# Seven block products for the value half of the first feed-forward too, and the key/value norm four tiles later

## What is computed

```
up = x @ w_up                      # (tokens, 1024) @ (1024, 2*2816)
u, val = up[..., :2816], up[..., 2816:]
c = conv_b + sum_j conv_w[j] * u_shifted[j]        # width 3
f = (gelu(c) * val) @ w_down       # (tokens, 2816) @ (2816, 1024)
h = h + rms_norm(f, g_ffn_post)
```

## Time and profile before

| | |
|---|---|
| median of three runs | 2568.37 us (2568.36 to 2572.23) |
| the profiled execution, its own time | 2568.32 us |
| its span, first to last instruction | 2566.5 us |
| mean granted TensorE clock | 0.986 of full |
| PE busy | 2434.8 us, 95% |
| DVE busy | 1752.6 us, 68% |
| ACT busy | 1190.4 us, 46% |
| down products of pass f = 0 | from 614.63 us |
| down products of pass f = 1 | from 988.29 us |
| down products of pass f = 2 | from 1810.88 us |
| down products of pass f = 3 | from 2181.33 us |

### The profile page before, as it was taken

One profiled execution on the slowest core, in us unless ns is written; L12 is line 12 of the kernel. 1 busy time (PEld: TensorE's weight loads), 2 busy tenths in 40 slices (PEclk: granted clock), 3 DMA queues, 4 the chain that ended last, 5 costly groups with the idle time before them and its releaser, 6 DMA issues. The chain is left out here.

```text
span 2566.5 us, 38650 instructions
## 1 busy us (share of the span) xinstructions
PE 2434.8 (95%) x15615; PEld 2140.6 (83%) x15615; DVE 1752.6 (68%) x3158; ACT 1190.4 (46%) x1884; POOL 44.1 (2%) x66
## 2 busy tenths in 40 slices
PE   7999999989999999999998899989899999999996
PEld 4777989877888889999996677767788889999996
DVE  5667576676766556766656655665888887787777
ACT  4655454454343334343325766764534544433343
POOL 0000000000000000000000000000000000000000
PEclk9999999999999999999999999989999999999998
DMA  4222223332433332423323242221333333233322
GB/s 160 66 66 91 83 79 108 120 108 88 161 102 117 105 99 89 134 75 99 109 83 92 96 126 64 85 79 54 92 116 134 99 99 99 84 106 124 99 91 98
DMA packets 88205, 255.24 MB, mean 99 GB/s; under 512 B 12963, under 2 KB 30540, under 8 KB 86092
## 3 DMA queue, kind: packets, MB, share of 16 engines
q1 hardware_dynamic: 68956, 202.45, 24.9%
q0 software_dynamic: 5792, 28.05, 3.4%
q10 hardware_dynamic: 13280, 22.28, 2.6%
HBM read 225.93 MB, written 26.74 MB: 98 GB/s over the span
## 5 line engine op out<-in xcount | busy, mean ns | idle before, releaser
L513 PE MATMUL banks<-act_hi,w_lo 128*128 128x272 f32 (+1 forms) x2520 | 834.5, 331 | 18.9 <-DVE act_lo L2634 7.3
L513 PE MATMUL banks<-act_hi,w_hi 128*128 128x272 f32 (+1 forms) x2520 | 819.8, 325 | 0.0
L513 PE MATMUL banks<-act_lo,w_hi 128*128 128x272 f32 (+1 forms) x2520 | 818.3, 325 | 0.0
L490 ACT ACTIVATE w_hi<-w_raw 128x1024 fp32r<-128x1024 f32 x366 | 382.5, 1055 | 575.2 <-PE banks L536 302.0
L496 DVE TENSOR_TENSOR w_lo<-w_raw,w_hi 128x1024 fp32r<-128x1024 f32 x366 | 444.2, 1221 | 235.9 <-ACT w_hi L490 235.6
L513 PEld LDWEIGHTS banks<-act_hi,w_lo 128*128 128x128 f32 x2520 | 477.3, 189 | 74.0 <-issue 24.6
L513 PEld LDWEIGHTS banks<-act_lo,w_hi 128*128 128x128 f32 x2520 | 478.0, 190 | 36.5 <-issue 1.7
L513 PEld LDWEIGHTS banks<-act_hi,w_hi 128*128 128x128 f32 x2520 | 476.7, 189 | 37.5
L548 DVE TENSOR_TENSOR acc<-acc,banks 128x272 f32<-128x272 f32 (+1 forms) x624 | 314.3, 518 | 182.8 <-PE banks L536 180.4
L536 PE MATMUL banks<-h_hi,w_lo 128*128 128x272 f32 (+1 forms) x1056 | 346.9, 328 | 21.9 <-DVE w_lo L496 8.3
L536 PE MATMUL banks<-h_lo,w_hi 128*128 128x272 f32 (+1 forms) x1056 | 345.4, 327 | 0.0
(11 more groups left out here) (275 smaller groups left out, 3430.3 us busy)
## 6 DMA issues: line engine op xcount, KB each, us to landing
w_raw<-wall SPq DMA_DIRECT2D x366, 512.0 KB, 3.5
normed<-h_scratch POOLq DMA_DIRECT2D x20, 352.0 KB, 4.1
h_scratch<-acc POOLq DMA_DIRECT2D x3, 2176.0 KB, 7.9
h_scratch<-acc POOLq DMA_DIRECT2D x3, 2048.0 KB, 7.8
gstates<-state ACTq DMA_DIRECT2D x4, 1024.0 KB, 6.4
gla_s<-gstates ACTq DMA_DIRECT2D x4, 1024.0 KB, 7.1
bias<-bias_scratch ACTq DMA_DIRECT2D x28, 128.0 KB, 2.9
bias_scratch<-bias_rows ACTq DMA_DIRECT2D x8, 383.0 KB
```

Source lines behind the costliest of these rows:

```text
L490: nc.scalar.activation(WH[:, b % RING, 0:n], raw(b), ACT.Copy).then_inc(w_hi, 1)
L513: last = nc.tensor.matmul(PS[:, bank, 0:n], w, a[X][:, k, o:o + n], start=(k == 0 and first), stop=(k == KT - 1 and w is wh and a is AH))
```

## The change

`SEVEN` becomes (0, 1, 2, 3) and `seven(f, g)` true for g >= 2, in pass f = 1 only for g <= 6: the seven products are made in nine pairs of f = 0 and five of f = 1 as well. `KV_TILE` goes from 13 to 17. The tile `bias_rows` is placed after everything that the feed-forward uses. The step tables of layer 0 become those of layer 1; the steps of the norm for keys and values (Sum, Root, n, hi, l) come four tiles later. The waits that guard shared tiles and banks are extended to the first layer: `act_sums` waits for the stores of the linear attention's states, and POOL's loads of the residual for the activation sums. In pass f = 0 the transfers of `bias_rows` stay at the odd tiles 3 to 17, seven of them now inside ACT's `seven_tile`.

```diff
--- before.py
+++ after.py
@@ -69,13 +69,13 @@
 NBW = 2 * WIN + 1
 RING, RAW = 3, 2
 KH = KT // 2
-KV_TILE = 13
-SEVEN = (2, 3)
+KV_TILE = 17
+SEVEN = (0, 1, 2, 3)
 
 
 def seven(f, g):
 
-    return f in SEVEN and g >= 2
+    return g >= 2 and (f != 1 or g <= 6)
 
 
 
@@ -278,7 +278,6 @@
         SEL = place("select", [P, SAMP])
         EL = place("gel", [P, 16])
         TM = place("masked_scores", [P, 2, HP // 2])
-        RB = place("bias_rows", [NQ, RL])
         gla_end = at[0]
 
 
@@ -331,6 +330,8 @@
         TR = place("sums_raw", [P, 4, KH, WM // 2], offset=at[0])
         TL = place("sums_lo", [P, 4, KH, WM // 2], fp32r)
         VX = place("w_sums", [P, 2, KH * P])
+        at[0] = max(at[0], gla_end)
+        RB = place("bias_rows", [NQ, RL])
         assert at[0] <= nc.sbuf_top, at[0]
         assert max(gla_end, att_end) <= nc.sbuf_top, (gla_end, att_end, nc.sbuf_top)
 
@@ -442,6 +443,7 @@
         GLRC = tally([(X, c) for X in range(2) for c in range(len(CHUNKS[X]))])
         TILE = tally([(f, t, c) for f in range(4) for t in range(FT) for c in range(len(CHUNKS[f % 2]))])
         VALS = tally([(f, t, c) for f in range(4) for t in range(FT) if not seven(f, t // 2) for c in range(len(CHUNKS[f % 2]))])
+        LAST_SEVEN = {f: max(g for g in range(FG) if seven(f, g)) for f in SEVEN}
         SEVENS = tally([(f, g) for f in range(4) for g in range(FG) if seven(f, g)])
         LOADED = [b for b in range(NW) if names[b][0] not in ("vs", "v4")]
         RAWI = {b: r for r, b in enumerate(LOADED)}
@@ -1399,22 +1401,17 @@
         FFN_I, FFN_PASS = (1, 1, 3, 3), ((1, 1), (2, 0), (3, 1), (4, 0))
 
 
-        PE_FFN = ({3: "sum", 9: "Sum"}, {3: "sum", 13: "Sum"})
-        DVE_SEVEN = ({1: ("f0",), 2: ("f1",), 7: ("a0", "a1"), 9: ("a2", "a3")}, {})
+        PE_FFN = {3: "sum", 13: "Sum"}
         DVE_AMID = {6: ("s0", "s1"), 8: ("s2", "s3"), 10: ("F0",), 12: ("F1",), 14: ("n0a", "n0b"), 16: ("l0a", "l0b"),
                     18: ("n1a", "n1b"), 20: ("l1a", "l1b")}
-        ACT_SEVEN = ({1: ("sq1",), 3: ("root",), 9: ("Sq0",), 10: ("Sq1",), 13: ("Root",), 15: ("hi0",), 19: ("hi1",)},
-                     {0: ("sq0",)})
-
-        DVE_FFN = ({1: ("f0",), 2: ("f1",), 4: ("s0", "s1"), 5: ("a1", "s2", "s3"), 6: ("a3",), 7: ("F0",), 8: ("F1",),
-                    10: ("n0a", "n0b"), 11: ("l0b", "n1a"), 13: ("l1b",)},
-                   {4: ("a0",), 5: ("a2",), 10: ("l0a",), 11: ("n1b",), 12: ("l1a",)})
-        ACT_FFN = ({1: ("sq1",), 3: ("root",), 6: ("Sq0",), 7: ("Sq1",), 9: ("Root",), 10: ("hi0",), 12: ("hi1",)},
-                   {0: ("sq0",)})
-
-        def ffn_steps(tables, f, t):
-
-            table = tables[f // 2]
+        DVE_FFN = {1: ("f0",), 2: ("f1",), 7: ("a0", "a1"), 9: ("a2", "a3")}
+        DVE_FFN_KV = ({**DVE_FFN, 14: ("n0a", "n0b"), 15: ("l0b", "n1a"), 17: ("l1b",)},
+                      {14: ("l0a",), 15: ("n1b",), 16: ("l1a",)})
+        ACT_FFN = {1: ("sq1",), 3: ("root",), 9: ("Sq0",), 10: ("Sq1",), 13: ("Root",), 15: ("hi0",), 19: ("hi1",)}
+        ACT_FFN_KV = {**ACT_FFN, 14: ("hi0",), 15: (), 16: ("hi1",), 19: ()}
+
+        def ffn_steps(table, f, t):
+
             return [(*FFN_PASS[f], name) for name in table.get(t, ())
                     if f < 3 or name[0] in "fsah" and name[:2] != "hi" or name == "root"]
 
@@ -1463,8 +1460,9 @@
                     pe_products(pe, f, t // 2)
                 return
             pe.wait_ge(w_lo, BLK["val", f, t] + 1)
-            if t == 0 and seven(f - 1, FG - 1):
-                pe.wait_ge(vp_read, 8 * SEVENS[f - 1, FG - 1])
+            before = (f, t // 2 - 1) if t else (f - 1, FG - 1)
+            if t % 2 == 0 and seven(*before):
+                pe.wait_ge(vp_read, 8 * SEVENS[before])
             for c in range(n):
                 if t - 3 + n >= 0:
                     pe.wait_ge(h_made, TILE[f, t - 3 + n, c])
@@ -1472,7 +1470,7 @@
                     pe.wait_ge(h_made, TILE[f - 1, FT - 2 + c, 0])
                 project(pe, X, BLK["val", f, t], c, 2 + (t % 2 if n == 1 else c), val_full)
 
-        PE_NAMES = [{t: (name,) for t, name in table.items()} for table in PE_FFN]
+        PE_NAMES = {t: (name,) for t, name in PE_FFN.items()}
 
         def tokens(X, j):
 
@@ -1533,7 +1531,7 @@
                 group = ffn_group(f, t)
                 if group is None:
                     continue
-                if t in (4, (10, 14)[f // 2]) and (t == 4 or f < 3):
+                if t in (4, 14) and (t == 4 or f < 3):
                     i, X = FFN_PASS[f]
                     pe.wait_ge(ms_done, NORMS[i, "post" if t == 4 else next_kind(i), X])
                 if f == 1 and t == KV_TILE + 1:
@@ -1698,11 +1696,14 @@
                 whole, made = [TP[:, i, :, 0:n] for i in range(2)], [TR[:, i, :, 0:n] for i in range(4)]
                 late = [NM[X][:, :, tokens(X, j)] for j in range(2)]
                 if k == 0:
-                    dve.wait_ge(al_done, 2 * ACTS[3, "pre", X])
-                    if f == SEVEN[0]:
+                    dve.wait_ge(al_done, 2 * ACTS[FFN_I[f], "pre", X])
+                    if f == 0:
+                        dve.wait_ge(gp_out, 16 * H)
+                        dve.wait_ge(st_out, 16 * H)
+                    else:
+                        dve.wait_ge(vp_full, 7 * SEVENS[f - 1, LAST_SEVEN[f - 1]])
+                    if f == 2:
                         dve.wait_ge(kw_out, 16 * 20)
-                    else:
-                        dve.wait_ge(vp_full, 7 * SEVENS[SEVEN[0], FG - 1])
                 if k < 2:
                     x = tokens(X, k)
                     nc.vector.tensor_tensor(whole[k], AH[X][:, 0:KH, x].bitcast(fp32), AL[X][:, 0:KH, x].bitcast(fp32),
@@ -1723,7 +1724,7 @@
                 g = t // 2
                 if t % 2 == 0:
                     far = 1 + f % 2
-                    amid = ffn_steps((DVE_AMID, DVE_AMID), f, t)
+                    amid = ffn_steps(DVE_AMID, f, t)
                     conv_before(f, t)
                     for m in range(8 * far):
                         down_add(dve, f % 2, (f, g - 1), m, 4 + m % 4, False)
@@ -1742,7 +1743,7 @@
                     for x in range(2):
                         rest_after(dve, ("d", f, g - 1, x))
                     return
-                for step in ffn_steps((DVE_FFN[0], DVE_SEVEN[0]), f, t):
+                for step in ffn_steps(DVE_FFN_KV[0] if f == 1 else DVE_FFN, f, t):
                     dve_step(dve, *step)
                 early, even, odd_tile = read_products(f, g)
                 rest_after(dve, ("u", f, t))
@@ -1775,7 +1776,7 @@
                 if f == 1 and t == KV_TILE:
                     for x in range(2):
                         rest_after(dve, ("kv", 0, x))
-                for step in ffn_steps((DVE_FFN[1], DVE_SEVEN[1]), f, t):
+                for step in ffn_steps(DVE_FFN_KV[1] if f == 1 else {}, f, t):
                     dve_step(dve, *step)
                 if f == 1 and t in (KV_TILE + 1, KV_TILE + 2):
                     dve_lo(dve, 2, "mix", 0, t - KV_TILE - 1, 0)
@@ -1855,10 +1856,12 @@
 
                 g = t // 2
                 bias(f, t)
-                for step in ffn_steps((ACT_FFN[0], ACT_SEVEN[0]), f, t):
+                for step in ffn_steps(ACT_FFN_KV if f == 1 else ACT_FFN, f, t):
                     act_step(act, *step, 6)
                 if f == 3 and t == 10:
                     act_y_store(act)
+                if f == 0 and t in range(3, 19, 2):
+                    bias_rows(t - 3)
                 if t % 2 == 0:
                     if t == 4:
                         sums_hi(f)
@@ -1912,7 +1915,7 @@
                 C = CB[:, t % 2]
                 act.wait_ge(cv2, FT * f + t + 1)
                 nc.scalar.activation(C[:, 0:cv], C[:, 0:cv], ACT.Gelu_apprx_tanh).then_inc(gl, 1)
-                for step in ffn_steps((ACT_FFN[1], ACT_SEVEN[1]), f, t):
+                for step in ffn_steps({0: ("sq0",)}, f, t):
                     act_step(act, *step, 6)
                 group = ffn_group(f, t)
                 if group is not None:
@@ -2750,8 +2753,8 @@
         def _(gp):
 
             for i, X in PASSES[1:]:
-                if i >= 3 and (i, X) != (3, 0):
-                    gp.wait_ge(t_hi, 10 * (i - 3) + 6)
+                if (i, X) in FFN_PASS:
+                    gp.wait_ge(t_hi, 10 * FFN_PASS.index((i, X)) + 6)
                 for y in range(4):
                     h_load(gp, i, X, y)
                 if i < 4:
```

## The result

The changed kernel takes 2615.89 us (median of 4 runs, 2613.44 to 2618.77), the kernel before beside it 2569.8 us (4 runs, 2568.36 to 2572.23): 1.0179 times as long, 95% interval 1.0161 to 1.0196. It is slower, and by more than the forecast of 2586.4 us and its range. The profiled execution took 2615.39 us, with a span of 2613.6 us against 2566.5.

What follows compares the result with a forecast made beforehand. It took TensorE, busy 95% of the span, as the bound. Pass 0 at -0.70, pass 1 at -5.71 and the bias-row transfers at +24.5 gave +18.1 us on the 2566.5 us span, so 2586.4 us; range 2567 to 2606 us.

Steps and rivals of the forecast that it cites:

- the loads behind the bias rows: Pass 0, seven pairs: weight loads land late behind bias-row transfers and delay the down products; 2586.4 us, chance 0.62.
- the loads have room: Rival: in pass 0 the down products do not wait for the late loads; 2562 us, chance 0.11.
- the term of the bias rows: Seven pairs of pass 0: 2.65 us idle plus 0.85 us of clock loss each, 24.5 us in all.
- The landing: Second weight load after the bias transfer's start (B) lands at B + 14.2, leaving TensorE 2.65 us idle a pair.
- the rival of the mild lateness: Pass 0: first load starts later, so the second may get through sooner; 0.7 to 1.3 us a pair, chance 0.09.
- the rival of the late slot: Pass 0: all second loads land at B + 16.7, with clock loss; 6.85 us a pair, 2610 us, chance 0.18.
- The clock: After idle time in pass 0's pairs the clock falls, costing 1.7 us, taken for half the pairs: 0.85 us each.
- Pass 0's stretch: From pair 0's down products to the last pair's, pass 0 takes pass 2's time: 338.31 to 335.11 us, -3.20.
- Ahead of it: From the mixer's down products to pair 0's in pass 0: 26.52 to 29.02 us, +2.50.
- pairs 9 and 10 would fall to 32.31 us: Sign to look for: these pass 0 pairs fall to 32.31 us, while pairs 2 to 8 take about 35 to 36.
- Pass 1: Pairs 0 to 5 save 10.75 us, the next interval takes 41.99 in place of 36.95, +5.04; in all -5.71 us.
- The norm of the keys and values four tiles later: Same steps on ordinary tiles, moved with the key/value blocks and hidden by the end of the pass: 0 us.

Runs made afterwards that it cites:

- e1: The changed kernel with its eight bias-row transfers cut as 16 rows by 16 copies, not two rows by 128: 2571.84 us, ratio 1.0010.
- e6: e1 with seven of its eight bias-row transfers moved from pass 0 to tiles 14 to 20 of pass 1: 2566.38 us, ratio 0.9983.
- e5: e1 with ACT's steps of tile 13, among them the norm's root, placed after the tile's last ACT work: 2570.88 us, ratio 1.0000.
- e8: e7 with ACT's steps of tile 13, the norm's root among them, late in all passes but pass 1: 2559.31 us, ratio 0.9960.
- e2: The kernel before with its bias-row transfers cut as in e1: 2569.12 us, ratio 0.9998.
- e3: The changed kernel with the bias rows in four transfers of four rows instead of eight of two: 2630.02 us, ratio 1.0236.
- e10: The changed kernel with the bias rows in two transfers of eight rows (tiles 3 and 11), timed once: 2598.7 us.
- e4: The changed kernel with seven two-row bias transfers started in the next pair's even tile, after its gelu: 2590.07 us, ratio 1.0082.
- e7: e6 with DVE's activation sums later, two at the end of tile 2 and four in tile 3: 2561.73 us, ratio 0.9969.

## Why the prediction was right in direction and wrong in size

*The forecast's likeliest case, the loads behind the bias rows, is what happened*: one gap a pair at the first down product, in six of the seven behind DVE's w_lo and ACT's wait for DMA. e1 and e6 show that without it 44 to 50 us are gone. The rival "the loads have room" is refuted.

*The step that failed is the size of the term of the bias rows*, "per pair 3.5 us, for seven 24.5 us". It measured 47.4 us, 6.8 a pair, in three parts:

- The landing. I had taken the second load at B + 14.2 from rows where both loads started earlier. There the first, issued at B + 2.2, had its 52 packets of wait behind it at B + 9.4. In the new pair (B = 871.27) the loads start at B + 4.4 and B + 7.9, the two engines come to them at B + 11.9, and the second lands at B + 15.8, in the other plain pairs at B + 15.8 to B + 17.0. The later first load, which the rival of the mild lateness had counted as a help, is what makes it later. The five plain pairs idle for 3.85 to 4.46 us, 4.1 in the mean, in place of 2.65: +7.1 us.
- The two pairs with more in them. The store of the stream and the steps of tile 13 were named in the rival of the late slot ("come on top") and priced nowhere. They idle for 8.94 and 6.47 us: +10.1 us over 2.65 each. The seven gaps together make 35.8 us in place of 18.6. One of them is in e6 too, with 1.84 us, which leaves the 33.9.
- The clock. I had let it fall in half the pairs at 1.7 us. It stood at 0.50 (the 1.2 GHz level) at every one of the seven gaps, for 3.4 us at three, 6.8 at three and 10.2 at one. The four longer ones start inside the gap, so that 3.4 to 5.9 us of work fall on the low clock each time; the matmuls of pass 0 took 13.5 us more than in e6, where I had 6.

So the time lay beyond my range, near where the rival of the late slot and the low clock had put it (2610 us). Its 6.85 us a pair are the measured 6.8, in part by luck: it had all second loads land at B + 16.7, and of the five in plain pairs they landed at 15.8 to 16.2 in three, at 16.5 and 17.0 in two; the rest of its sum came from the two pairs that it had only named. The idle time is 4.8 of the 6.8 us and the clock 1.9, for 5.15 and 1.7.

*Pass 0's stretch*, forecast at -3.20 us by pass 2's, came to -0.17 in e6 (338.14 for 338.31). Of the 3.0 us, 1.5 are in the interval behind the one with the store of the stream (33.92 us for 32.39 in pass 2) and 1.1 in that one (35.56 for 34.46). *Ahead of it*, +2.50 was forecast and +2.48 measured (617.11 - 614.63). The sign that pairs 9 and 10 would fall to 32.31 us was misread from the start for pair 10, which takes 38.78 us in pass 2 of the kernel before; for pair 9 the clock left over from the last gap made it 35.07.

*Pass 1*: from pair 0 to pair 5 177.35 us, 177.17 forecast. The next interval takes 44.81 us, 41.99 forecast. The forecast had the norm's steps there at DVE's 0.84 us and did not see ACT's, whose root and its tables take 4 us: TensorE stands still for 1.28 us behind ACT, in the tile of the root.

```profile
1242.46 0.36 PE L1491 MATMUL banks<-act_hi,w_lo 128*128 128x272 f32 x1 [1.28 <-ACT hf L1876]
```

e5 shows it: with these steps late the interval takes 42.27 us. Pass 1 in all: -2.7 us for -5.7.

*The norm of the keys and values four tiles later*: the tile with it takes 48.13 us, 48.15 before. Behind the pass, to the first down products of pass 2, +0.9 us. The price of 0 holds within that; it was not run by itself. *The new waits*: nothing idles at them in the profile; not run by themselves either.

*The clean sum.* Without the bias rows' term the forecast had a span of 2560.1 us (2566.5 - 6.4). The profiled execution of e6, the nearest to it, has 2568.2: 3.0 of the 8.1 us are pass 0's stretch, 3.1 pass 1's, 1.0 the time ahead of pass 0, and 1.1 the rest. This execution is 3.7 us above the median of e6, so the parts are those of one of the longer executions; by the medians (2566.4 against 2562) the difference is 4.4 us. So without the slow transfers the change as built lies between 3 us lost (e1) and 3 us won (e6), and it takes the later sums and the later root of e8 to make 10 us of it.

## What to carry to other kernels

A transfer of few bytes can be the dearest in the kernel: what counts for the loads of other queues is how many DMA engines it uses, how many packets each gets, and how fast its source gives them. Put a dimension of 16 outermost, over rows of several groups of four partitions, so that every engine has few packets (e1), and look for stretches in which the DMA share stands at a sixteenth or two while a load is under way. And where a change takes TensorE time out of a loop, price every transfer of that loop anew against the shorter chain: the old kernel's indifference to it (e2) says nothing.

When a stall is priced, add what it does to the clock, and price the pairs that have more in them by themselves. Two of seven made 15.4 of 35.8 us here.

## What the runs showed of the hardware

- Transfers of 0.2 to 1.6 MB make the first 512 KB load behind them, in a plain seven-product pair, take 3.7 to 17.1 us, by their shape. 2, 4 and 8 engines give 9.6, 16.9 and 17.1 us (g = 5 or 7), since four rows share one source and each engine's packets take twice as long; 16 engines give 3.8 us, with four groups of four rows, and 5.6 us with one row.
- An engine busy with such a transfer sends 51 to 53 more of its packets before the first of a load that has begun on the other engines, in 3.5 to 12.8 us by their rate. Then the two alternate, one packet each (33 and 32 in 3.3 us on two engines).
- 1532 B packets from one to four neighbouring partitions leave at 16 to 19 per us together, in the mean of 7 to 8 us; from 8 at 32, from 16 at 68, from two that are 8 apart at 27. For one us two neighbouring ones gave 34.
- At every gap of TensorE of 3.3 us or more in pass 0 the granted clock fell to 0.50, in the changed kernel for 3.4 to 10.2 us, in e3 and e10 for up to 13.7 us, starting inside the gap or within 1 us of its end. Shorter gaps are undecided: 1.84 us (e6), 2.39 us (e4) and 2.66 us (e7, pass 2) had a fall of 3.4 us at them, 2.36 us (e4) and 2.64 us (e7, pass 0) had none.
